# Three pieces of token columns, 416 + 416 + 256 in place of 364 + 364 + 360, in a two-layer decoder step

## The reference

```
mix = ...
x = _layer_norm(DN_ALPHA * x + g1 * mix, ln_g[layer, 0], ln_b[layer, 0])
h = x * (1.0 + sc2) + sh2
f = jnp.square(jax.nn.relu(h @ w_up[layer])) @ w_down[layer]
x = _layer_norm(DN_ALPHA * x + g2 * f, ln_g[layer, 1], ln_b[layer, 1])
```

## Time and profile before

| | us |
|---|---|
| median of 3 runs | 3541.26 |
| lowest and highest of the runs | 3541.24, 3542.87 |
| profiled execution | 3548.3 |
| span of the profiled execution | 3546.6 |

### The profile page before, as it was taken

How to read it: one execution, slowest core, us unless ns; L and a number is a source line. 1 busy time by engine, 2 the same in 40 slices (tenths; PEclk the granted TensorE clock), 3 DMA queues, 4 the chain that set the end, 5 groups by cost and what they waited for, 6 DMA issues and landing times. The chain is left out here.

```text
span 3546.6 us, 55400 instructions
## 1 busy us (share of the span) xinstructions
PE 3182.0 (90%) x20656; PEld 2678.5 (76%) x20656; DVE 1949.7 (55%) x3429; ACT 966.6 (27%) x1682; POOL 438.5 (12%) x248
## 2 busy tenths in 40 slices
PE   5556999999998997799999997888798999999997
PEld 1235999999997997766666564444497999999995
DVE  2466555555555112266666666888735555555554
ACT  0106000000004002144444445777634000000003
POOL 0001112212211211100000000000021112212210
PEclk8778999999999998899999998999999999999999
DMA  8630111111110221399999993000010111111101
GB/s 336 233 99 24 40 38 47 47 41 47 47 48 13 89 67 51 134 385 408 407 409 407 407 406 112 25 25 19 24 49 22 40 40 47 47 41 47 47 25 51
DMA packets 215688, 433.93 MB, mean 122 GB/s; under 512 B 13664, under 2 KB 130057, under 8 KB 212441
## 3 DMA queue, kind: packets, MB, share of 16 engines
q1 hardware_dynamic: 215521, 431.67, 33.3%
HBM read 417.92 MB, written 13.92 MB: 122 GB/s over the span
## 5 line engine op out<-in xcount | busy, mean ns | idle before, releaser
L73 PE MATMUL bank<-hi,mlp_uphi 128*128 128x364 f32 (+1 forms) x1536 | 510.2, 332 | 45.5 <-DVE lo L413 28.8
L74 PE MATMUL bank<-lo,mlp_uphi 128*128 128x364 f32 (+1 forms) x1536 | 507.5, 330 | 0.0
L75 PE MATMUL bank<-hi,mlp_uplo 128*128 128x364 f32 (+1 forms) x1536 | 507.2, 330 | 0.0
L73 PE MATMUL bank<-mlp_fhi,mlp_dnhi 128*128 128x364 f32 (+1 forms) x1536 | 506.9, 330 | 0.0
L74 PE MATMUL bank<-mlp_flo,mlp_dnhi 128*128 128x364 f32 (+1 forms) x1536 | 504.8, 329 | 0.0
L75 PE MATMUL bank<-mlp_fhi,mlp_dnlo 128*128 128x364 f32 (+1 forms) x1536 | 504.6, 329 | 0.0
L291 DVE SCALAR_TENSOR_TENSOR x_t<-bank,mod,x_t 128x364 f32<-128x364 f32 (+1 forms) x432 | 245.6, 571 | 378.1 <-PE bank L75 376.1
L73 PEld LDWEIGHTS bank<-hi,mlp_uphi 128*128 128x128 f32 x1536 | 291.2, 190 | 49.7 <-issue 47.7
L1581 PE MATMUL bank<-ident,sa_kraw 128*128 128x128 f32 x2048 | 277.6, 280 | 47.0 <-DMA sa_kraw<-in_cache_k 42.5
L1581 PEld LDWEIGHTS bank<-ident,sa_kraw 128*128 128x128 f32 x2048 | 225.7, 142 | 98.8 <-DMA sa_kraw<-in_cache_k 70.4
L74 PEld LDWEIGHTS bank<-lo,mlp_uphi 128*128 128x128 f32 x1536 | 291.2, 190 | 0.3
(11 more groups left out here) (269 smaller groups left out, 5491.1 us busy)
## 6 DMA issues: line engine op xcount, KB each, us to landing
sa_kraw<-in_cache_k SPq DMA_DIRECT2D x256, 512.0 KB, 10.6
sa_vpage<-in_cache_v SPq DMA_DIRECT2D x256, 512.0 KB, 9.4
mlp_raw<-in_w_up SPq DMA_DIRECT2D x64, 512.0 KB, 4.0
mlp_raw<-in_w_down SPq DMA_DIRECT2D x64, 512.0 KB, 3.4
w_raw<-in_w_ada SPq DMA_DIRECT2D x24, 1024.0 KB, 8.2
pm_wada<-in_w_ada SPq DMA_DIRECT2D x48, 512.0 KB, 5.3
kv_raw<-in_w_kv SPq DMA_DIRECT2D x8, 1024.0 KB, 5.6
x_rows<-in_x_prompt SPq DMA_DIRECT2D x1, 4096.0 KB, 13.9
```

The costliest lines, as they stand in the source:

```text
L73: pe.matmul(out, w_hi, x_hi, start=start, stop=False, skip_group_check=True)
L74: pe.matmul(out, w_hi, x_lo, start=False, stop=False, skip_group_check=True)
L75: return pe.matmul(out, w_lo, x_hi, start=False, stop=stop, skip_group_check=True)
```

## The change

The table of pieces becomes 416, 416 and 256 columns, and with it the prompt part of the last piece goes from 296 to 192 columns. Three buffers that hold one piece grow to 416 columns, and two that lie behind them move. No instruction is added or removed, and each engine's instructions stand in the same order as before; those that work on one piece change their width.

```diff
--- before.py
+++ after.py
@@ -20,8 +20,9 @@
 H, HD = 16, 64
 DFF = 4096
 PAGES = 32
-PIECES = [(0, 364), (364, 364), (728, 360)]
-LASTP = TP - 728
+WIDE = 416
+PIECES = [(0, WIDE), (WIDE, WIDE), (2 * WIDE, T - 2 * WIDE)]
+LASTP = TP - 2 * WIDE
 ALPHA = 4.0 ** 0.25
 EPS = 1e-5 / ALPHA ** 2
 MASKED = -1e30
@@ -325,7 +326,7 @@
         self.gain, self.bias = k.ln_g[layer][which], k.ln_b[layer][which]
         self.sq = k.at("norm_sq", [P, NC, T], F32, k.HH_AT)
         self.h = k.at("norm_h", [P, NC, T], F32, k.HH_AT + NC * T * 4)
-        self.rstd = k.at("norm_rstd", [P, 364], F32, k.WORK_AT + 60544)
+        self.rstd = k.at("norm_rstd", [P, WIDE], F32, k.WORK_AT + 57344 + 8 * WIDE + 256)
         (self.mu, self.centred, self.squared, self.var, self.eps, self.inv, self.root, self.scaled, self.high, self.normed,
          self.split, self.coef, self.dve_own) = signals(
             name, "mu", "centred", "squared", "var", "eps", "inv", "root", "scaled", "high", "normed", "split", "coef",
@@ -473,8 +474,8 @@
         self.up_lo = k.at("mlp_uplo", [P, 2, NC, P], F32R, o + 16384)
         self.dn_hi = k.at("mlp_dnhi", [P, self.FC, D], F32R, o + 24576)
         self.dn_lo = k.at("mlp_dnlo", [P, self.FC, D], F32R, o + 40960)
-        self.f = k.at("mlp_f", [P, 2, 364], F32, o + 57344)
-        self.tmp = k.at("mlp_tmp", [P, TS], F32, o + 57344 + 2912)
+        self.f = k.at("mlp_f", [P, 2, WIDE], F32, o + 57344)
+        self.tmp = k.at("mlp_tmp", [P, TS], F32, o + 57344 + 8 * WIDE)
         self.f_hi = k.at("mlp_fhi", [P, self.FC, T], F32R, k.F_AT)
         self.f_lo = k.at("mlp_flo", [P, self.FC, T], F32R, k.F_AT + self.FC * T * 4)
         self.w_hi_done, self.w_done, self.job_done, self.bank_free, self.dve_own = signals(
@@ -1143,7 +1144,7 @@
         w_hi = k.at("proj_hi", [P, 2, NC, P], F32R, o + 8192)
         w_lo = k.at("proj_lo", [P, 2, NC, P], F32R, o + 16384)
         tmp = k.at("proj_tmp", [P, TS], F32, o + 24576)
-        h_full = k.at("proj_h", [P, 2, NC, 364], F32, o + 24832)
+        h_full = k.at("proj_h", [P, 2, NC, WIDE], F32, o + 24832)
         w_hi_done, w_done, job_done, bank_free, dve_own, h_done, h_split = sems(
             ctx, nc, name, "w_hi_done", "w_done", "job_done", "bank_free", "dve_own", "h_done", "h_split")
         raw_in = sems(ctx, nc, name, "raw_in0", "raw_in1")
```

## The result

| | median, us | runs | ratio to before, 95% interval |
|---|---|---|---|
| before | 3541.36 | 6 | |
| changed | 3555.85 | 6 | 1.0044 [1.0031, 1.0057] |

The change is slower: its median is 14.5 us (0.41%) above that of before. The forecast was +12.6 us.

What follows compares the result with a forecast made beforehand. PE was taken as the bound: busy 90% of the span, without gap in the MLPs. Stream -4.6, job 6 +17.3 and joins -0.1 sum to +12.6 us, from 3541.3 to a median of 3553.9; range 3534 to 3574.

Steps and rivals of the forecast that it cites:

- The stream: Matmuls in MLPs, pool mixer and projections: 3504 triples (one weights set, three pieces) go from 499.3 to 498.0 ns, -4.6 us.
- T: Distance from matmul to matmul at 416 columns, not shown by any profile row; taken as 189.0 ns.
- Rival A: Streams of all MLPs: per-matmul overhead is fixed, T is 186.7, giving back 20.7 us; 3537.8 in all, chance 0.22.
- Job 6: MLP blocks: the shorter last piece no longer covers ACT and POOL's weights chain, PE waits 1.15 us, 15 times: +17.3 us.
- Joins: Norms and stage joins: columns the same in sum, cover moves between pieces; about -0.1 us, -8 to +8.
- the forecast's own test: The two MLP stretches should grow by about 13 us together, or the forecast is wrong.
- n00: Norm ahead of layer 0's MLP: up jobs start after wider pieces, last piece waits less; +1.5 us, 0 to +4.
- n01: Norm behind layer 0's MLP: waits for the means of middle and last piece grow; +4.2 us, 0 to +8.
- n10: Norm ahead of layer 1's MLP: the last piece's exposed chain gets shorter; -3.8 us, -6 to 0.
- n11 and the tail: Norm behind layer 1's MLP, to the end: less exposed behind the last mean, longer waits ahead; -2.0 us, -6 to +4.
- Rival B: Each new 1.2-us hole at job 6 halves PE's clock behind it: +24 us more, 3578; chance 0.12.
- Rival C: At job 6 POOL's half comes sooner, the hole is half a microsecond: +7 for +17.3, 3544; chance 0.08.

Runs made afterwards that it cites:

- e3: The changed kernel with pieces 432/432/224 in place of 416/416/256, old order of up jobs: 3578.53 us, 1.0099 of before.
- e4: The changed kernel with pieces 384/384/320 in place of 416/416/256, old order of up jobs: 3532.82 us, 0.9972 of before.
- e6: The changed kernel with pieces 352/384/352 in place of 416/416/256, old order of up jobs: 3535.21 us, 0.9980 of before.
- e1_order: The changed kernel (416/416/256) with up jobs reordered, chunk by chunk, in all blocks but each layer's first: 3544.34 us, 1.0006 of before.
- e2_order_364: The kernel before (364/364/360) with up jobs reordered, chunk by chunk, in all blocks but each layer's first: 3542.11 us, 0.9996 of before.
- e10: The changed kernel with pieces 320/416/352 in place of 416/416/256, old order of up jobs: 3535.70 us in one run, before 3540.91.

## Why the prediction held, and where it didn't

1. **The stream** (-4.6 us forecast). T came out at 188.3 to 190.0 ns against the 189.0 chosen, and the term at 3504 x -1.0 = -3.4 us. That the value fits is luck: e3, e4 and e6 show that distances don't lie on a line, for 224 columns have 111.6 ns where it gives 106, and 384 have 173.3 or 176.0 where it gives 175. Rival A's 186.7 is what a clean 416 would have had; 416 wasn't clean from any of the three starts tried. By the rule that the Trainium skill (TensorE: Matmul & The Clock Gate, Back-to-back issue gap) gives for an isolated matmul, 416 and 256 columns would have an estimated 175.8 and 109.2 ns; the stream in the trace has 189 and 120, and the measurement decides.
2. **Job 6** (+17.3 us forecast). Shown by e1_order, which takes the wait away and the loss with it, and by the waits at three widths. The term was too large: the block's growth of 0.73 and the 0.19 that its stream gave back make 0.92 per block in place of 1.15, 15 x 0.92 = 13.8 us. The mis-sized step is "POOL still ends about 3.95 us after job 5's start": it ended after 3.74, since POOL took 2.40 us in place of 2.61, which the bound of 0.2 allowed. And PE followed 0.05 us behind it, as it already did in the earlier trace rows; the 0.14 of the earlier trace rows comes in the first and the last block of a layer alone. So the two MLPs grew by about 11 us by their blocks, where the forecast's own test had about 13.
3. **Joins** (-0.1 us forecast). n00, n01 and n10 came out within 1.5 us each (the stretches with them: +0.8, +6.5, -4.1 for +1.3, +5.1, -3.2). n11 and the tail failed: "-2.0, between -6 and +4" is +2.1 (the stretch's 2.8 less the block's 0.7). Two parts of the step: the clock behind the longer wait, 1.7 us, which I had read in n01 and not carried to n11, and the wider pieces' means and variances, which I took at 1.1 outside of waits. Four such groups of 52 columns more each, 0.65 us apiece on the timeline, are 2.6. Behind the last mean 0.9 us less came back than the 6.2 forecast; most of that is not laid to rows, but the mean itself went from 7.2 to 6.5 us only. That the length of the wait decides the clock is not shown. In n11 e2_order_364, with the old pieces, kept 1.00 as before did, and e1_order, with the new ones, fell as the change did; the last section has waits of one length with either clock.

So +12.6 was near +14.5 partly because two errors of opposite sign, about 3.5 and 4 us, met. Rival B's clock came in the norms but not in job 6. The stretch behind the hole of block 1 (its job 6 starts at 432.79), the granted clock third from the end:

```profile
432.80:436.00 3.20, 3.20 (x17) 3.18 (x18) 3.10 (x5) 0.00 (x0) 2.48 (x1) 1.00 0.51 148
```

The granted clock is 1.00. Rival C's faster POOL came, by the 0.2 us above, but its hole of half a microsecond and its "+7" did not: the seven waits sum to 5.4 us.

## What to carry to other kernels

When tiles are re-cut, go through each producer that hides behind one short tile, and hold its time against the new time of that tile: here 3.95 us behind 4.00 had no slack to give. That time is not quite fixed: POOL's same subtraction took between 2.37 and 2.62 us in blocks 1 to 6, by the kernel. Try cuts whose widths and starts are multiples of 64 columns before reasoning about balance; of the two orders of 320, 384 and 384 that were tried with a wide last piece, the better one had the small piece first. Around a norm the last piece counts twice: a shorter one leaves less exposed behind the last mean (37.9 us before, 32.6 after) and covers less ahead of it (a wait of 6.58 before, 7.78 after).

## What the runs showed that I had not expected

- Matmuls of one width have more than one distance: 384 columns had 176.0 ns from column 352 and 173.3 from column 384, and 352 columns from column 736 had 158.4 and 166.6 in blocks of one kernel (e10).
- DVE's subtraction on 128 x 256 took 2.56 us beside POOL's in the change, where one on 128 x 416 took 0.59 alone, 2.5 us earlier. It ends 0.27 us behind POOL's subtraction (529.43):

```profile
524.68 0.59 DVE L563 TENSOR_TENSOR mlp_flo<-mlp_f,mlp_fhi 128x416 fp32r<-128x416 f32 x1
...
527.14 2.56 DVE L563 TENSOR_TENSOR mlp_flo<-mlp_f,mlp_fhi 128x256 fp32r<-128x256 f32 x1
```

- In n11, the granted clock behind PE's wait for DVE was 1.00 after waits of 1.00 and 1.95 us, 0.70 after 2.21 and 0.59 after 3.77. The length alone is no rule for it: in n01 of the kernel before, the same 1.95 us were followed by 0.50, and in e6_352_384_352 a wait of 1.85 us was followed by the full clock in n01 and by a lower one in n11. The two stretches of e6, n01 first:

```profile
1075.60:1080.40 4.80, 4.80 (x17) 2.81 (x16) 1.34 (x5) 4.77 (x10) 0.00 (x0) 1.00 0.01 3
3466.30:3472.80 6.50, 6.50 (x17) 3.56 (x16) 1.31 (x5) 3.89 (x7) 0.00 (x0) 0.74 0.00 0
```

  The stretches are of unlike length, so the figures between 0.50 and 1.00 can't be held against each other. What the falls shown cost can: 3.2 x 0.50, 4.1 x 0.41, 5.7 x 0.30 and 6.5 x 0.26 are 1.6 to 1.7 us each. It is no constant: in n01 of the change 7.8 us at 0.67 are 2.6.
